# Banded attention on one core: scores, maximum, exponential and scaling run one tile deeper, and GpSimd makes seven low parts in the last pair

## The reference, cut to what matters

```python
def odd_layer(h, w_in, b_in, sinks, w_out):
    proj = h @ w_in + b_in
    q, k, v, g = jnp.split(proj, ODD_SPLITS, axis=-1)
    ...
    o = sliding_window_attention(q, k, v, sinks, alibi_slopes(SW_HEADS))
    return (o * jax.nn.silu(g)) @ w_out

# inside sliding_window_attention: a block of 128 queries sees its own
# block of keys and the one before; 16 heads of 64, 2 key/value heads
    logits = jnp.einsum('bnqkgd,bnskd->bnkgqs', qb, kk).astype(jnp.float32) * scale
    logits = logits - sl * dist.astype(jnp.float32)
    logits = jnp.where(valid[None, :, None, None], logits, -jnp.inf)
    p = jax.nn.softmax(jnp.concatenate([logits, sink], axis=-1), axis=-1)[..., :-1]
    out = jnp.einsum('bnkgqs,bnskd->bnqkgd', p.astype(v.dtype), vv)
```

## Time and profile before

| | us |
|---|---|
| median of 3 runs | 2469.41 |
| lowest, highest | 2464.82, 2470.40 |
| the profiled execution, its own time | 2468.76 |
| its span, first to last instruction | 2466.9 |
| TensorE busy over the span | 2368.4 (96%) |
| VectorE, ScalarE, GpSimd busy | 1493.0, 1220.0, 185.2 |

### The profile page before, as it was taken

One profiled execution on the slowest core, in us unless ns is written; L12 is line 12 of the kernel. 1 busy time (PEld: TensorE's weight loads), 2 busy tenths in 40 slices (PEclk: granted clock), 3 DMA queues, 4 the chain that ended last, 5 costly groups with the idle time before them and its releaser, 6 DMA issues. The chain is left out here.

```text
span 2466.9 us, 31321 instructions
## 1 busy us (share of the span) xinstructions
PE 2368.4 (96%) x11991; PEld 1953.2 (79%) x11991; DVE 1493.0 (61%) x2739; ACT 1220.0 (49%) x2205; POOL 185.2 (8%) x112
## 2 busy tenths in 40 slices
PE   7999899998999999999999999999999999999988
PEld 6777687887888777788888887888787787888776
DVE  6767756536656657655555555653476665666665
ACT  5545633224545544666666555332455434656552
POOL 0000021000000043000000000000112030000022
PEclk9999999999999999999999999999999999999999
DMA  3222422112221332111110111224434431111143
GB/s 130 81 73 81 137 92 75 66 66 81 89 89 53 112 106 69 49 39 43 35 43 26 43 35 35 85 102 177 170 127 159 137 94 55 35 52 45 47 136 120
DMA packets 93135, 203.05 MB, mean 82 GB/s; under 512 B 10368, under 2 KB 45568, under 8 KB 91968
## 3 DMA queue, kind: packets, MB, share of 16 engines
q1 hardware_dynamic: 92992, 201.12, 24.3%
HBM read 160.13 MB, written 40.96 MB: 82 GB/s over the span
## 5 line engine op out<-in xcount | busy, mean ns | idle before, releaser
L224 PE MATMUL acc<-operand_hi,w_hi 128*128 128x512 f32 (+1 forms) x1814 | 733.3, 404 | 31.9 <-DVE operand_lo L370 9.5
L226 PE MATMUL acc<-operand_hi,w_lo 128*128 128x512 f32 (+1 forms) x1814 | 711.1, 392 | 0.0
L225 PE MATMUL acc<-operand_lo,w_hi 128*128 128x512 f32 (+1 forms) x1814 | 709.9, 391 | 0.0
L224 PEld LDWEIGHTS acc<-operand_hi,w_hi 128*128 128x128 f32 x1814 | 343.5, 189 | 109.2 <-issue 22.3
L226 PEld LDWEIGHTS acc<-operand_hi,w_lo 128*128 128x128 f32 x1814 | 343.1, 189 | 74.2
L225 PEld LDWEIGHTS acc<-operand_lo,w_hi 128*128 128x128 f32 x1814 | 344.0, 190 | 67.1 <-issue 3.3
L192 DVE TENSOR_TENSOR w_lo<-w_raw,w_hi 128x1024 fp32r<-128x1024 f32 (+2 forms) x203 | 228.3, 1125 | 175.3 <-ACT w_hi L186 173.0
L186 ACT ACTIVATE w_hi<-w_raw 128x1024 fp32r<-128x1024 f32 (+2 forms) x203 | 197.2, 972 | 277.1 <-PE aux L226 141.9
L224 PE MATMUL aux<-operand_hi,w_hi 128*128 128x512 f32 x618 | 250.1, 405 | 20.6 <-DVE resid L3238 5.0
L226 PE MATMUL aux<-operand_hi,w_lo 128*128 128x512 f32 x618 | 242.6, 393 | 0.0
L225 PE MATMUL aux<-operand_lo,w_hi 128*128 128x512 f32 x618 | 242.1, 392 | 0.0
(11 more groups left out here) (463 smaller groups left out, 3848.4 us busy)
## 6 DMA issues: line engine op xcount, KB each, us to landing
w_raw<-in_stream SPq DMA_DIRECT2D x201, 512.0 KB, 3.6
ssd_e<-cs_scratch SPq DMA_DIRECT2D x8, 1024.0 KB, 6.8
g_scratch<-ssd_work SPq DMA_DIRECT2D x12, 512.0 KB, 2.9
ssd_xbc<-g_scratch SPq DMA_DIRECT2D x8, 768.0 KB, 4.9
y_scratch<-rnn_y SPq DMA_DIRECT2D x10, 512.0 KB, 2.6
out_a_raw<-y_scratch SPq DMA_DIRECT2D x19, 256.0 KB, 4.4
resid<-in_x SPq DMA_DIRECT2D x8, 512.0 KB, 8.7
g_scratch<-mlai_g SPq DMA_DIRECT2D x8, 512.0 KB, 2.9
```

The lines of the kernel that those rows point to most:

```text
L224: pe.matmul(out, w_hi, x_hi, start=first, stop=False)
L225: pe.matmul(out, w_hi, x_lo, start=False, stop=False)
L226: return pe.matmul(out, w_lo, x_hi, start=False, stop=last)
```

## The change

On TensorE the scores of tile n+2 move from the end of iteration n to right behind the transposes of n, ahead of the quarter of the projection. The first tile's scores of the next pair stay at the end of iteration 6, the second tile's go behind the transposes of 7. On VectorE the maximum of n+2 (was n+1) comes first, then the work beside, then the scaling of n+1; at n = 6 the scaling comes first and the maximum of the next pair's tile 0 last. ScalarE takes the exponentials of n+2 (was n+1). The tanh moves from n = 0 to n = 2 and the gate's product from n = 0 to n = 3; the slopes move from n = 2 to n = 3. In the last pair the low parts 0 to 6 go from VectorE to GpSimd; the eighth stays on VectorE, at n = 7, behind a wait for the seven.

```diff
                 mm.then_inc(s["pt"], 1)
+                if n + 2 < QT:
+                    pe_scores(pe, p, par, n + 2, None)
+                elif n + 1 == QT and not last:
+                    pe_scores(pe, p + 1, 1 - par, 1, nxt[0])
                 if not last:
...
-                if n + 2 < QT:
-                    pe_scores(pe, p, par, n + 2, None)
-                elif not last:
-                    pe_scores(pe, p + 1, 1 - par, n + 2 - QT, nxt[0])
+                if n + 2 == QT and not last:
+                    pe_scores(pe, p + 1, 1 - par, 0, nxt[0])
...
         act_exp(act, 0, 0)
+        act_exp(act, 0, 1)
...
-                if n + 1 < QT or not last:
-                    act_exp(act, p if n + 1 < QT else p + 1, (n + 1) % QT)
+                if n + 2 < QT or not last:
+                    act_exp(act, p if n + 2 < QT else p + 1, (n + 2) % QT)
                 if n == 0:
                     act.wait_ge(s["y"], groups * p)
                     act_gate(act, g_tile(i, par), p)
+                if n == 2:
+                    act_tanh(act, g_tile(i, par))
...
-                if n == 2 and not last:
+                if n == 3 and not last:
                     act_slopes(act, p + 1, 1 - par)
...
         dve_max(dve, 0, 0)
+        dve_max(dve, 0, 1)
         dve_norm(dve, 0, 0)
+
+        def beside(i, par, p, n, last):
+            if n in (2, 7) and not last:
+                split_lo(dve, k, g_tile(i, par + 1) if n == 2 else q_tile(i, par + 2))
+            if n in (5, 6) and not last:
+                dve_queries(dve, q_tile(i, par + 1), p + 1, 1 - par, n - 5,
+                            k.acc[:, q_tile(i, par + 1).slot, :])
+            if n == 3:
+                dve.wait_ge(s["tanh"], p + 1)
+                dve.scalar_tensor_tensor(out=g[:, :], in0=tg[:, :], scalar=1.0, in1=g[:, :],
+                                         op0=ALU.add, op1=ALU.mult).then_inc(s["gate"], 1)
+            if last and n == 0:
+                split_lo(dve, k, begun.tile(1))
...
+                if n + 2 < QT:
+                    dve_max(dve, p, n + 2)
+                elif n + 2 > QT and not last:
+                    dve_max(dve, p + 1, 1)
+                if n + 2 == QT:
+                    dve_norm(dve, p, n + 1)
+                beside(i, par, p, n, last)
+                if n + 2 == QT and not last:
+                    dve_max(dve, p + 1, 0)
+                if n + 2 < QT:
+                    dve_norm(dve, p, n + 1)
+                elif n + 2 > QT and not last:
+                    dve_norm(dve, p + 1, 0)
+                if last and n == QT - 1:
+                    dve.wait_ge(begun.s["lo"], SW_PAIRS - 1)
+                    begun.low(dve, SW_PAIRS - 1, y[:, 0:HALF])
+                    split_lo(dve, k, begun.tile(2))
                 if n % GROUP == GROUP - 1:
+                    if n < GROUP:
+                        dve.wait_ge(s["gate"], p + 1)
+                        dve.wait_ge(s["stored"], 16 * p)
                     dve.wait_ge(s["pv"], N // GROUP + 1)
...
+    @block.gpsimd
+    def _(pool):
+        for d in range(SW_PAIRS - 1):
+            begun.low(pool, d)
```

More of the change, by code:

```diff
@@ L3507, in act_gate, with act_tanh @@
                        bias=k.vec[:, bass.ds(VEC["b_g"] + p, 1)]).then_inc(k.acc_free[t.slot], 1)
+    def act_tanh(act, t):
         act.wait_ge(k.acc_free[t.slot], t.before + 1)
```

## The result

The changed kernel took 2473.12 us, the median of 21 runs (2467.02 to 2475.00); beside it the kernel before took 2468.30 us, the median of 21 runs (2463.45 to 2471.98). The ratio of the runs is 1.0016 with a 95% interval of 1.0010 to 1.0023: 3.9 us more, between 2.5 and 5.7 (the two medians differ by 4.8). The forecast was 2471.8 us, a change within 0.2% of the time, and a range of 2464 to 2478: the measured 0.16% and 2473.12 us agree with it, though the interval, 0.10 to 0.23%, reaches a little over 0.2%. The prediction also took it that so small a change could not be told from none; 21 runs of each kernel do tell it.

The account below looks back on a forecast made before the run. TensorE was taken to bound the middle pairs, a three-engine chain the last. +2.7 us for seven pairs and -0.3 for the last made +2.4, on a median of 2469.41: 2471.8 us, range 2464 to 2478.

Parts of the forecast that it names:

- What bounds: In middle pairs TensorE, where only idle time can be won; in the last pair a chain over three engines.
- Part 1, the loop: Seven pairs: VectorE's work between maximum and scaling delays transposes of tiles 3 and 6; +2.7 us, bounds 0.6 to 4.8.
- the two links that no row of before showed: Maximum's small sum to next operation, and scores behind transposes in projection pairs: 0.15 us either way per stalled tile.
- Part 2, the last pair: Last pair with seven low parts on GpSimd: 34.8 us against 35.1, taken as -0.3; bounds -2.0 to +3.5.
- the paragraph on the shared port: GpSimd and VectorE exclude each other for some operations; GpSimd's low parts fall where VectorE waits for scores, costing nothing.
- a two-port mode: From the skill text: GpSimd contends with VectorE where VectorE reads two SBUF inputs or runs in this mode.
- The depth does its work: Rival: the loop doesn't bind at n = 2 and 5, all stalls go, 2457 us; 13 in 100 including a half case.
- GpSimd holds up scaling: Rival: in the last pair late GpSimd low parts delay VectorE's small sum, 6.5 us over five tiles, 2478; 12 in 100.
- The loop is longer than priced: Rival: both parts reach their bounds together, +4.8 and +1.5, giving 2475.7 us; 10 in 100.
- The waiting of VectorE for seven low parts: Last pair, n = 7: GpSimd done at about 30.1 us, TensorE reaches the eighth at 31.4; costs nothing.

Follow-up runs that it names:

- e3: The changed kernel with VectorE's scaling of n+1 ahead of the work beside in every iteration but the seventh: 2458.48 us, ratio 0.9962 to the kernel before.
- e4: The changed kernel with scaling ahead of the low weights at n = 2 alone: 2467.10 us, ratio 0.9992 to the kernel before.
- e1: The changed kernel without GpSimd, all eight low parts of the last pair on VectorE: 2470.45 us, ratio 1.0010 to the kernel before.
- e2: The kernel before with only the seven low parts of the last pair moved to GpSimd: 2473.93 us, ratio 1.0024 to the kernel before.
- e7: The changed kernel run again with nothing altered, for a second profile: 2472.45 us, one execution.
- e8: The changed kernel with the first four loads of y for the output projection issued one pair earlier: 2473.48 us, one execution.
- e5: e3 with all eight low parts of the last pair on VectorE in place of GpSimd: 2457.54 us, ratio 0.9955 to the kernel before.

## Why the prediction was right, and where a term was mis-sized

**What bounds.** Right. The middle pairs stayed TensorE's, and only its idle time moved.

**Part 1, the loop.** Right in place and nearly in size. Predicted 4.34 and 4.65 us for the stalled tiles, measured 4.32 and 4.62 (over the 3.68 of e3 that is 0.64 and 0.94; the idle times that the trace puts down to VectorE are 0.48 and 0.78, not the 0.7 and 1.0 foretold); predicted pair 35.24, measured 35.20 to 35.22; +2.7 us for seven pairs, measured +2.28. Of the two links that no row of before showed, the scores behind transposes were as in the earlier trace rows, 1.12 us to the maximum. With nothing beside, the maximum to scaling is 1.01 (2137.42 to 2138.43) where I took 1.13; this loop doesn't bind, so nothing depended on it. The first tile takes 3.75 us, 0.09 more than I kept for it; its transposes now follow the values directly and take 0.66 us in place of 0.60, which is most of it. e3 and e4 show the cause, not only its place. VectorE no longer waits for ScalarE's exponentials in the list of waits, as foretold.

**Part 2, the last pair.** Predicted 34.8 us, measured 36.41; -0.3 should have been +1.3. By its own steps:

| from T(0) | T(1) | T(2) | T(3) | T(4) | T(5) | T(6) | T(7) | end |
|---|---|---|---|---|---|---|---|---|
| predicted | 7.1 | 11.0 | 14.3 | 20.2 | 23.5 | 26.9 | 29.6 | 34.8 |
| measured | 8.12 | 12.45 | 15.68 | 21.69 | 24.92 | 28.16 | 31.22 | 36.41 |

1.0 of the 1.6 us is there at T(1) and 0.4 more comes by T(2), in the stretch at half clock (e1 has the same 4.33 us from T(1) to T(2), where I took 3.9); then the steps are within 0.2 us of the prediction, among them 6.01 us from T(3) to T(4) with a product waiting 1.39 for GpSimd, against 5.9, but for T(6) to T(7), 3.06 against 2.7, where a product waits 0.91 for GpSimd. e1, the same order without GpSimd, has T(1) at 7.07: the chain that I added up to 7.1 was right, and the 1.05 us on it is the held scaling.

**The step that failed** is the sentence in the paragraph on the shared port that a GpSimd low part "lies where VectorE waits for scores, so it costs nothing". It had two errors. It looked only at tiles in their regular pace and not at n = 0, where the split of weights puts the scaling late and the load of `y` puts the subtraction there too. The prediction's own times for n = 0 had them meet: the scaling's first operation at 7.1 - 1.07 = 6.0, and the low part done at 8.0, so begun at 6.2 to 6.7; the trace has 6.01, and 6.66 to 7.92. And it took only VectorE's operations with two SBUF inputs for exposed, the small sums, while the trace now shows that the scaling, with one tensor input, is held as well. The Trainium skill, SBUF — State Buffer, section "Who interferes with whom", states that tensor_scalar can enter a two-port mode that contends with GpSimd, and that whichever is issued first then keeps the pair for its whole instruction, the other fully blocked. The runs agree (a scaling of 0.35 held to 1.41 us). In the other direction, GpSimd's subtraction of 1.26 us was held to 1.78 by the low weights, which have two SBUF inputs. My sentence on "a two-port mode" was not followed to the instruction that it applies to.

The same port was met three more times in the last pair of the changed kernel, with little or no delay of a transpose: sums of 0.38 and 1.25 us at n = 3, and a scaling of 1.68 at n = 6. That they cost little is seen in that T(4) and T(7) follow what TensorE's products wait for, not the scaling.

**The rivals.** "The depth does its work" did not come, for the reason given (the order on VectorE), and e3 shows that it comes when the order is changed. "GpSimd holds up scaling" came at a cost once in eight tiles instead of in five, for 1.05 us, and under another condition than the one given: GpSimd's low parts took 1.26 to 1.31 us, not over 1.8. That e2's 6.3 us are close to the 6.5 worked out for this rival is luck: 1.4 of them lie behind T(7), at the lower clock, and the five tiles cost 4.35. "The loop is longer than priced" was not so; its price took +1.5 us for the last pair where the bound of part 2 is +3.5, so the sum 2475.7 does not follow from the two bounds. The waiting of VectorE for seven low parts cost 1.3 us of its idle time and nothing of TensorE's, as priced.

**The size of the whole.** 3.58 us against a sum of 2.4: 0.4 too much in part 1, 1.6 too little in part 2, errors that partly cancel. That the forecast time is only 1.3 us from the measured one is in part luck as well, since the kernel before came out 1.1 us under the median that it was added to (2468.30 against 2469.41).

## What to carry to other kernels

When a chain is made one tile deeper, look for the loop that the engine's fixed order closes: what stands between taking the new tile's input and finishing the old tile's work is inside the loop, and it was free before only because the engine was waiting there. Put the operation that another engine needs first and the work beside behind it; here this one reordering turned +2.3 us into -8.4. And before work goes to GpSimd, list VectorE's operations on the critical path that can meet it, those with one SBUF input and a scalar too, and price one meeting at up to GpSimd's whole instruction (1.05 us here, of 1.26).

## What the runs showed of the hardware that I had not expected

- A scaling of 128x256 with one tensor input in SBUF (0.35 us) is held by a GpSimd subtraction of two SBUF inputs until that ends: 1.35 to 1.43 us over all runs with GpSimd. A sum of two elements is held just as long (1.22 to 1.28 in place of 0.15). 0.1 us in the start decides. The maximum, which reads its scores from PSUM, is not held: 0.48 us at 2361.11 of the profile after, inside the subtraction of 2360.72 to 2362.00. In the profile before, scalings of this kind take 0.49 us for 512 columns and 0.75 for 1024, 0.52 ns a column, and subtractions with two SBUF inputs 0.69 and 1.23, 1.06 ns a column.
- GpSimd's subtraction of 128x512 is steady when nothing meets it: 1.26 to 1.31 us in the changed kernel, against a median of 1.81 of its additions in the earlier trace rows. VectorE does the same in 0.69.
- The clock differs between executions of the same instructions. In every profile TensorE is idle for 2.08 us in the stage's start, and then the start takes 11.0 us or 12.6 (after, e2, e7). The windows of the same stretch, before and then after, with the granted clock as the third number from the end:

```profile
2072.00:2076.00 4.00, 4.00 (x19) 3.28 (x18) 1.03 (x1) 3.95 (x4) 0.00 (x0) 1.00 0.57 180
```

```profile
2072.00:2076.00 4.00, 3.90 (x11) 3.20 (x12) 0.83 (x2) 3.88 (x4) 0.00 (x0) 0.64 0.59 177
```

  The 1.57 us in the comparison of the two profiles is this, and is no effect of the change: e8, whose code is that of the changed kernel there, has 11.0, and e2, whose attention begins as before, 12.6. In the three slow starts the clock fell to 1.2 GHz only 0.4 to 1.2 us after the idle time had ended, while TensorE worked. Likewise in the last pair: after 2.1 us of idle before T(1), e5's transposes took 1.11 us, at 1.2 GHz, and e3's 0.66, at 2.4; e3's clock fell 2.9 us behind T(1), in the next wait. After the long wait for T(1), 6.99 us, the changed kernel ran on at half clock:

```profile
2352.00:2356.00 4.00, 4.00 (x14) 3.40 (x14) 1.91 (x9) 2.09 (x7) 0.00 (x0) 0.50 0.20 66
```

  Why one execution loses the clock after 2.1 us and another doesn't is left open; with 1.57 us it can be one part of the several us over which the runs of one kernel spread.
